# Twelve gate groups and four modulation chunks move from HGRN's end into RWKV's rounds

## The reference, cut to what matters

```python
mod = cs @ p['w_ada'] + p['b_ada']                 # modulation: 6 x 1024 columns for 9 sequences
sh1, sc1, gt1, sh2, sc2, gt2 = jnp.split(mod, 6, axis=-1)
h = modulate(h_res, p['g_mix'], sh1, sc1)
z = h @ p['w_in']
u_a, p_b, q_c, f_c, i_c, og_c, gate_logits = jnp.split(z, IN_SPLITS, axis=-1)
y_a, ... = s5_mixer(u_a, ...)
y_b, ... = rwkv7_mixer(p_b, ...)
y_c, ... = hgrn2_mixer(q_c, f_c, i_c, og_c, ...)
gates = jax.nn.sigmoid(gate_logits).reshape(n, l, N_BRANCH, D_MODEL)
merged = (gates[:, :, 0] * (y_a @ p['w_lift_a']) + gates[:, :, 1] * (y_b @ p['w_lift_b'])
          + gates[:, :, 2] * (y_c @ p['w_lift_c']))
h_res = h_res + gt1[:, None, :] * (merged @ p['w_out'])
h2 = modulate(h_res, p['g_ffn'], sh2, sc2)
# then w_up, a short convolution, gelu, w_down, and the last norm
```

## Time and profile before

| | us |
|---|---|
| median of 3 runs (2611.31 to 2615.77) | 2615.44 |
| profiled execution | 2614.35 |
| its span | 2612.6 |

### The profile page before, as it was taken

The page is one execution under the profiler, slowest core; times in us unless marked ns, Lnnn a source line. Parts: engine busy times, 40 slices in busy tenths (PEclk is TensorE's granted clock), DMA queues, the critical chain, the costliest instruction groups (busy, mean ns, idle before and its releaser), DMA issues.

```text
span 2612.6 us, 40403 instructions
## 1 busy us (share of the span) xinstructions
PE 2350.0 (90%) x18161; PEld 1542.5 (59%) x18161; DVE 878.1 (34%) x1398; ACT 453.5 (17%) x894; POOL 158.5 (6%) x269
## 2 busy tenths in 40 slices
PE   5998999897897897887889997999999999999994
PEld 3665665565655556555556664666656666665663
DVE  3953441015315325324324333333330013323222
ACT  4115121113113123113120002111110001111002
POOL 2700000001001001001000000000000000000001
PEclk8999999999999999999979998999999999999997
DMA  7101223420020020020143211111100111111001
GB/s 225 63 21 42 80 99 100 157 71 16 11 60 16 11 60 17 13 65 16 39 153 109 81 33 33 33 33 46 46 25 24 57 33 34 33 34 42 20 21 67
DMA packets 111371, 139.81 MB, mean 54 GB/s; under 512 B 14818, under 2 KB 85975, under 8 KB 111184
## 3 DMA queue, kind: packets, MB, share of 16 engines
q1 hardware_dynamic: 96512, 115.38, 13.7%
q10 hardware_dynamic: 10992, 15.21, 1.6%
q0 software_dynamic: 3696, 6.64, 0.9%
HBM read 117.59 MB, written 19.61 MB: 53 GB/s over the span
## 4 chain that ended last, share of the span: by engine, by line
PE 80%; DVE 8%; ACT 4%; issue 4%; DMA 3%; POOL 0%; ACTq 0%; SPq 0%; DVEq 0%; POOLq 0%
PE ps L629 79%; DVE arena L1740 3%; DMA W<-in_w_in_dram 2%; DVE arena L1743 2%; PE ps L633 1%; ACT Y L1495 1%; DMA arena<-in_x_prompt_dram 1%; ACT arena L1374 1%; POOL arena L586 0%; DMA Y<-in_x_prompt_dram 0%; DVE hT L1743 0%; DVE hT L1740 0%; DVE arena L2107 0%; ACT arena L1420 0%; DVE s5v L1740 0%
## 5 line engine op out<-in xcount | busy, mean ns | idle before, releaser
L629 PE MATMUL ps<-hT,W 128*128 128x352 f32 x4368 | 1356.5, 469 | 53.2 <-DMA W<-in_w_in_dram 16.6
L629 PEld LDWEIGHTS ps<-hT,W 128*128 128x128 f32 x4368 | 832.6, 193 | 517.9 <-issue 58.5
L629 PE MATMUL ps<-arena,W 128*128 128x352 f32 x1440 | 434.1, 465 | 14.7 <-DVE arena L1740 11.9
L629 PEld LDWEIGHTS ps<-arena,W 128*128 128x128 f32 x1440 | 277.1, 193 | 171.1 <-DVE arena L1740 12.5
L629 PE MATMUL ps<-arena 64*64 64x64 f32 (+5 forms) x9224 | 270.1, 229 | 64.5 <-issue 51.4
L629 PEld LDWEIGHTS ps<-arena 64*64 64x64 f32 (+2 forms) x9224 | 221.7, 134 | 140.4 <-issue 80.8
L1374 ACT ACTIVATE Y<-ps 128x352 f32<-128x352 f32 (+3 forms) x220 | 69.8, 350 | 716.1 <-PE ps L629 537.1
L2286 DVE TENSOR_SCALAR Y<-Y,PAR 128x1024 f32<-128x1024 f32 x88 | 49.0, 557 | 426.8 <-ACT Y L1374 425.2
L1740 DVE TENSOR_TENSOR arena<-arena 128x1056 f32<-128x1056 f32 (+6 forms) x181 | 166.8, 922 | 60.0 <-PE ps L629 45.0
L1374 ACT ACTIVATE arena<-ps 128x512 f32<-128x512 f32 (+6 forms) x179 | 106.3, 608 | 406.0 <-PE ps L629 202.4
L1740 DVE TENSOR_TENSOR arena<-ps,arena 128x512 f32<-128x512 f32 (+4 forms) x124 | 93.2, 751 | 223.3 <-PE ps L629 170.9
(11 more groups left out here) (252 smaller groups left out, 954.6 us busy)
## 6 DMA issues: line engine op xcount, KB each, us to landing
W<-in_w_ada_dram SPq DMA_DIRECT2D x12, 2048.0 KB, 9.4
W<-in_w_up_dram SPq DMA_DIRECT2D x22, 1024.0 KB, 7.1
gates<-arena ACTq DMA_DIRECT2D x72, 176.0 KB, 1.8
arena<-gates SPq DMA_DIRECT2D x24, 528.0 KB, 3.5
W<-in_w_in_dram SPq DMA_DIRECT2D x17, 512.0 KB, 5.4
W<-in_w_in_dram SPq DMA_DIRECT2D x4, 1536.0 KB, 7.2
W<-in_w_down_dram SPq DMA_DIRECT2D x4, 1536.0 KB, 6.8
W<-in_w_in_dram SPq DMA_DIRECT2D x5, 1024.0 KB, 6.5
```

Source lines behind the costliest of these rows:

```text
L629: return nc.tensor.matmul(out, lhsT, rhs, start=start, stop=stop, skip_group_check=True)
```

## The change

The loop of four chunks at HGRN's end is gone. Its twelve gate groups and its four modulation chunks (8 to 11) are spread over the four rounds of RWKV: a round now has a gate chunk of four tiles (twelve groups instead of nine) and one modulation chunk.

- In the levels, a piece of two matmuls (four records) stands behind each `yy(l + 1, s)`; these are groups 5 and 6. Group 7 is cut in four pieces between the steps behind the levels. The chunk loop holds groups 8 and 9, the decoding part group 10.
- At the round's end, group 11 is issued whole, then `ada_rows`, the sums, `ada_cols`. The half group that stood in front of the sums of squares is gone from there.
- So that banks 6 and 7 are free for the gates in the levels, the product with `KA` and `vb` (for `W0`) stands ahead of the levels, ScalarE copies it behind level 1, and `W0` has a place of its own (that of `Gm`). The later products use banks 0 to 3 instead of 6, 7 and 2, 3, and the one for `R` (`YT` and `LA`) is now the last ahead of the chunk loop.
- SyncE loads `rkv`, `gate`, `ada` for each round, and by the two slots the next round's `rkv` waits for the last gate group of this one. ScalarE copies the modulation's input once more (`cs32b`) in the first round.

```diff
@@ gate_tiles, weight_chunks
-    return (2 * c, 2) if c < 4 else (4 + c, 1) if c < 8 else (12 + 3 * (c - 8), 3)
+    return (2 * c, 2) if c < 4 else (8 + 4 * (c - 4), 4)
...
-        out += [("rkv", j, 3 * G), ("gate", 8 + j, 3 * G)]
+        out += [("rkv", j, 3 * G), ("gate", 4 + j, 4 * G), ("ada", 8 + j, 1)]
@@ TensorE, HGRN's end
-            ada_rows(7, 3)
-            for c in range(8, 12):
-                gate(3 * c)
-                ada_cols(c - 1, 5)
-                gate(3 * c + 1, 3 * c + 2)
-                ada_rows(c, 3 + (c + 1) % 2)
+            ada_rows(7, 6)
 
             i = index[("lora", 0)]
             arrived(i)
             gemm(wslot(i, 0, 8, 128), 0, 8, h, "z_ev")
-            ada_cols(11, 5)
+            ada_cols(7, 7)
@@ TensorE, levels
-                for l in range(1, last):
-                    for s in range(2):
-                        zx(l, s)
-                        zt(l, s)
-                        yy(l + 1, s)
                 pe.wait_ge(sem("la_ev"), 5 * (j + 1))
...
                 give("wy_ev", 6, 7)
-                for s in range(2):
-                    zt(last, s)
+                for l in range(1, last):
+                    for s in range(2):
+                        zx(l, s)
+                        zt(l, s)
+                        yy(l + 1, s)
+                        k = 4 * ((l - 1) % 2) + 2 * s
+                        gates_part(4 + j, 5 + (l - 1) // 2, k, k + 2)
+                zt(last, 0)
+                gates_part(4 + j, 7, 0, 2)
+                zt(last, 1)
                 pe.wait_ge(sem("tk_ev"), 6 * (j + 1))
                 for s in range(2):
+                    if s:
+                        gates_part(4 + j, 7, 2, 4)
                     pe.wait_ge(sem("zt_ev"), level_at(j, last, s))
...
@@ TensorE, ahead of the chunk loop
-                        m = mm(pb[2 + par_][hp, col64(c // 2)], YT[sd, pos(c), :], LA[sd, lane(c), 1, :])
-                m.then_inc(sem("gm_done"), 1)
-                give("gm_ev", 2, 3)
+                        mm(pb[2 + par_][hp, col64(c // 2)], vb(c, 0)[sd, :], KA[sd, lane(c), 1, :], c < 2, False)
+                        m = mm(pb[2 + par_][hp, col64(c // 2)], U0[sd, pos(c), :], LA[sd, lane(c), 1, :], False, False)
+                m.then_inc(sem("y_part"), 1)
+                gates_part(4 + j, 7, 6, KT)
                 take(0, 1)
...
+                        m = mm(pb[par_][hp, col64(c // 2)], YT[sd, pos(c), :], LA[sd, lane(c), 1, :])
+                m.then_inc(sem("gm_done"), 1)
+                give("gm_ev", 0, 1)
@@ TensorE, the round's end
-                gates_part(8 + j, 8, 0, 4)
+                gates_part(4 + j, 11, 0, KT)
+                pe.wait_ge(sem("cs_ready"), 2)
+                ada_rows(8 + j, 3)
                 pe.wait_ge(sem("ry_ev"), 2 * (j + 1))
...
                 give("sum_ev", 0, 1, 2)
+                ada_cols(8 + j, 4)
...
                 give("rw_rows", 7)
-                gates_part(8 + j, 8, 4, KT)
                 pe.wait_ge(sem("ysq_ready"), j + 1)
@@ SyncE, in a round
-                weights(index[("gate", 8 + j)])
+                weights(index[("gate", 4 + j)])
+                weights(index[("ada", 8 + j)])
@@ ScalarE, levels and the round's end
-                act.wait_ge(sem("wy_done"), 2 * j + 1)
-                copy(W0[:].rearrange("p c t -> p (c t)"), ps[:, 6:8, :].rearrange("p b t -> p (b t)"))\
-                    .then_inc(sem("wy_ev"), 1)
+                    if l == 1:
+                        act.wait_ge(sem("wy_done"), 2 * j + 1)
+                        copy(W0[:].rearrange("p c t -> p (c t)"), ps[:, 6:8, :].rearrange("p b t -> p (b t)"))\
+                            .then_inc(sem("wy_ev"), 1)
+                    if l == 3:
+                        save_gate(4 + j, 5, pb[7])
+                save_gate(4 + j, 6, pb[6])
...
+                save_gate(4 + j, 10, pb[6])
+                save_gate(4 + j, 11, pb[7])
+                ada_copy(8 + j, 3)
+                ada_mod(8 + j, 4)
                 act.wait_ge(sem("centred"), j + 1)
                 nc.scalar.activation(C2, C1, ACT.Square).then_inc(sem("ysq_ready"), 1)
-                save_gate(8 + j, 8, pb[6])
```

More of the change, by code:

```diff
@@ L76, in weight_chunks @@
     out += [("s5", 0, 2 * G), ("hg", 0, 4 * G), ("hg", 1, 4 * G)]
-    for c in range(8):
-        out += [("gate", c, gate_tiles(c)[1] * G), ("ada", 4 + c, 1)]
+    for c in range(4):
+        out += [("gate", c, 2 * G), ("ada", 4 + c, 1)]
     out += [("lora", 0, G)]
     for j in range(4):
-        out += [("rkv", j, 3 * G), ("gate", 8 + j, 3 * G)]
+        out += [("rkv", j, 3 * G), ("gate", 4 + j, 4 * G), ("ada", 8 + j, 1)]
     out += [("lift", c, 12) for c in range(2)]
@@ L321, in hg_group @@
         def hg_group(n):
-            return (n // 6, n % 6) if n < 24 else (n // 3 - 4, n % 3)
+            return n // 6, n % 6
         def half_of(h):
@@ L708, in ada_cols @@
                 pe.wait_ge(sem("ada_ev"), c + 1)
-                rows_, at = (adaT, 4 * c) if c < 4 else (adaT2, 0)
+                row = adaT[:, c % 2, :] if c < 4 else adaT2[:, c % 2, :] if c < 8 else adaT3
+                at = 4 * c if c < 4 else 0
                 if c >= 4:
@@ L1405, in ada_copy @@
                     act.wait_ge(sem("ada_done"), c - 1)
-                copy((adaT if c < 4 else adaT2)[:, c % 2, :], pb[b][:, :]).then_inc(sem("ada_ev"), 1)
+                row = adaT[:, c % 2, :] if c < 4 else adaT2[:, c % 2, :] if c < 8 else adaT3
+                copy(row, pb[b][:, :]).then_inc(sem("ada_ev"), 1)
             def ada_mod(c, b):
@@ L1557, in _ @@
                 gate(12 * t + 10, 12 * t + 11)
-            ada_copy(7, 3)
-            for c in range(8, 12):
-                gate(3 * c)
-                ada_mod(c - 1, 5)
-                gate(3 * c + 1, 3 * c + 2)
-                ada_copy(c, 3 + (c + 1) % 2)
+            ada_copy(7, 6)
             for k in range(3):
-                act.wait_ge(sem(f"gate_saved{k}"), 16 * 12)
+                act.wait_ge(sem(f"gate_saved{k}"), 16 * 8)
             act.wait_ge(sem("hg_done"), 2)
@@ L1584, in _ @@
                     z_evac(zplace(Z[1 + q]), ACT.Copy, signals[index[("rkv", j)]] + G * q)
+                if j == 0:
+                    act.wait_ge(sem("lora_mixed"), 2)
+                    copy(cs32b[:, :, 0:NSEQ], csT[:, :, :]).then_inc(sem("cs_ready"), 1)
                 act.wait_ge(sem("sin_done"), j + 1)
@@ L1629, in _ @@
                     .then_inc(sem("wy_ev"), 1)
-                for n in (5, 6):
-                    save_gate(8 + j, n, pb[6 + n % 2])
+                save_gate(4 + j, 7, pb[7])
+                save_gate(4 + j, 8, pb[6])
+                save_gate(4 + j, 9, pb[7])
                 act.wait_ge(sem("dec_done"), 7 * j + 1)
-                copy(dT[:].rearrange("p a b -> p (a b)"), pb[2][:, 0:192]).then_inc(sem("dec_copied"), 1)
+                copy(dT[:].rearrange("p a b -> p (a b)"), pb[0][:, 0:192]).then_inc(sem("dec_copied"), 1)
                 act.wait_ge(sem("dec_done"), 7 * j + 4)
@@ L2168, in _ @@
                     r = ARp[:, par_:16:2, 1, :]
[L2169 removed]
+                    step(tt(r, pb[par_].rearrange("p (c t) -> p c t", t=RCH), r, ADD), "gm_ev" if par_ else "dve_step")
                 for c in range(1, 16):
```

101 lines of the change are left out of this document (50 added, 51 removed).

## The result

| | before | after |
|---|---|---|
| median of four runs, us | 2614.23 (2611.31 to 2615.77) | 2590.86 (2589.27 to 2591.87) |
| profiled execution / span, us | 2614.35 / 2612.6 | 2590.91 / 2589.2 |
| mean granted TensorE clock | 0.961 | 0.960 |

The ratio is 0.9917, 95% interval 0.9903 to 0.993. Forecast were 2571 us (2551 to 2593) and a gain of 44 us; it came to 23.4.

What follows compares the result with a forecast made beforehand. TensorE, busy 90% of the span, was taken to bound the kernel, and arriving instructions its levels. 2614.35 - 84 + 4 x (6.1 + 3.7) + 1 = 2570.5, with 1.1 for the median 2571 us, range 2551 to 2593.

Steps and rivals of the forecast that it cites:

- What bounds the levels: RWKV's levels: they run as instructions arrive, one packet in 3.9 us, so pieces cost time only beyond that pace.
- Removed, -84: HGRN's end: the dropped loop of gate groups and modulation chunks, from 433.6 to 518.0 us, saves 84 us.
- A round's end, +3.7: End of each RWKV round: whole group 11, modulation and sums make 22.2 instead of 18.5 us, range 3.2 to 4.5.
- The levels, +6.1: Each round, XT's first product to the chunk loop: 47.5 instead of 41.4 us with twelve pieces added.
- In front, +0.3: Ahead of the levels: the 64 records on K and A add 0.3 us, mostly lying in ScalarE's 0.87 us.
- Half level 3.63: In the levels: 2.24 us plus a piece of 1.39 makes 3.63 us, and the breaks for instructions go.
- Behind the levels: From the levels to the chunk loop: 584 small records, four pieces and one new wait, taken as 18.0 us.
- The start, 0: From the kernel's start to the rows of chunk 7 at HGRN's end: no change, 0 us.
- The lower end of the levels' term: Levels' region: with pieces at 1.21 us and 15.5 us behind the levels, about +2.9 us a round.
- as forecast: Whole kernel: the main case, 2562 to 2580 us, chance 0.58.
- partly filled breaks: Levels' region: stretches with one piece or none still stop, or ScalarE's sigmoid delays a copy; +10, 2587 us, chance 0.18.
- Slower: Levels: breaks do not belong to instructions, each piece paid in full at 1.39 to 1.65 us; 2618 to 2631 us, chance 0.09.

Runs made afterwards that it cites:

- the wide columns: Kernel before, with 288 matmuls a round in and behind the levels streaming 128 columns of zeros instead of 64 of data: 2621.0 us, ratio 1.0008.
- the groups in front: Changed kernel, with gate groups 5, 6 and 7 of each round issued whole ahead of the `la` products instead of in pieces: 2617.96 us, ratio 1.0001.
- the repetitions: The changed kernel and the kernel before, each profiled once more without any edit: 2593.46 us and 2616.49 us.

## Why the prediction was right, and where its size was off

- **What bounds the levels: right.** Instruction fetch, one packet in 3.9 us; shown by the wide columns (27.0 us more of TensorE work, 1.3 us more of rounds) and by the groups in front (the gain gone).
- **Removed, -84: right** (-86.0; -2.0 more; -83.4 between the repetitions). The first group behind the wait ran at the full rate already, so my allowance for it was not needed.
- **A round's end, +3.7: right** (+3.8), with the wait of 6.45 still there. But the sum left it unused: the gaps of the first and third round hold the modulation for nothing, that of the fourth in part.
- **The levels, +6.1: the term that was mis-sized** (+9.4, and +11.0 between the two repetitions). In the first round, which has +12.4:
  - *In front, +0.3:* the first piece came 24.3 us behind the sums, in before the same place lies at 21.9: +2.4. I let the 64 records for W0 lie in ScalarE's wait of 0.87. They lie in a run of short records without any piece, and there a record costs its share of a packet, 64 x 3.91 / 126 = 2.0 us by estimate. Moving them back took 1.1 to 2.4 off the front, round by round. In this round the clock has a part too: it was 0.70 from 546.3 to 552.0, behind the sums, and 1.00 there in the repetition.
  - *Half level 3.63:* 3.80, seven times, +1.2. My 2.24 + 1.39 added a piece to a run whose records it splits; the split costs 0.17 more.
  - *Behind the levels:* 20.6 us from the last of the eight pieces to the chunk loop instead of 19.4, +1.2: the break of 1.11 at 612.65, on 212 records with no piece, on top of the wait of 1.60 that I had counted.
  - *The chunk loop,* not in the sum: 28.0 instead of 26.5 us in the first and second round, +1.5. The granted clock was 0.66 in its first 5 us. That the wait of 1.60 brings this about is not shown: in rounds 3 and 4 the loop takes 26.5 with the same wait, and the kernel before has 28.0 and 0.66 in its third round without any. Over all 13 profiles the loop was longer than 26.5 in 12 of 24 rounds with the wait and in 4 of 28 without it. So it comes more often with the wait, but also without; the cause stays open.

  2.1 + 1.2 + 1.2 + 1.5 = 6.0 of the 6.3 us between +12.4 and +6.1. This is one round of one execution: in the repetition its first piece came at 23.1 and its chunk loop took 26.5. The half levels and the part behind them are the same there within 0.3 us.
- **The start, 0: 10.4 us,** not a step of mine but the ground that the sum stands on: I took the profiled execution's stages as given. Repetitions of the two kernels take back 8.1 of the 10.4 (4.4 and 3.7), so in them the miss lies in the levels.
- **Smaller slips of the sum.** The lower end of the levels' term is +2.2 by its own numbers (29.5 - 8 x 0.18 + 15.5 - 41.4), not +2.9. And with the fourth run the median of the kernel before is 2614.23, 0.1 below the profiled execution and not 1.1 above it, which takes 1 us off the forecast.
- **The rivals.** The case "as forecast", 2562 to 2580, did not come; the range holds the result only because it was drawn past the partly filled breaks (2587, +10 a round), which came nearest. Half of their mechanism came too: the stretch behind the levels with one piece to 256 small records still stops, by 1.1 to 1.8 us in each round of both profiles. The other half did not: within the levels every break is filled. "Slower" fell: a piece costs 0.79 us net (9.4 / 12), or 0.92 between the repetitions, not 1.39 to 1.65.

## What to carry to other kernels

Where very short instructions stand dense, count instructions, not their time: put the long instructions evenly between them, first where the run is longest, and charge a short instruction moved into such a run with its share of a packet. Put a filler in front of the instruction that waits, not behind it, and look at every round's gap by itself before giving all rounds the same order. Before you sum up from one execution's stages, ask for a second one.

## What the runs showed of the hardware

- TensorE took dense 64x64 float32 products at about one 16 KB packet of instructions in 3.9 us (252 instructions, 126 records; the earlier trace rows); with twice the columns in 288 of the matmuls 11 packets came in 44 us.
- Four records of 128x352 between 64x64 ones take 1.38 us from start to start (566.69 to 568.07) and 1.21 among their like. The Trainium skill, page "TensorEngine Tiling (Array Packing)", section "Key Properties", has the engine drained at a change of mode; 0.17 us for a piece, two changes, agrees with that. Whether the drain is its cause was not tried.
- 32 records of `zt` take 598.56 to 599.64 = 1.08 us, where 64 records of the `la` products take 1.16 (545.70, in the kernel with W0 moved back). `zt` writes one bank only; whether that is the cause was not tried.
